# Column-band attention: filler products ahead of PE's waits, the first pair turned in the projection, negated scores, the edge table built between steps

## What is computed

```python
def odd_mixer(x, w_qkv, rel_bias, w_o):
    q, k, v = jnp.split(x @ w_qkv, 3, axis=-1)        # 16 heads of 64
    o = neighbourhood_attention(q.reshape(shp), k.reshape(shp), v.reshape(shp), rel_bias)
    return o @ w_o
...
        k_win = k_band[:, :, :, col_idx]              # 16 columns around each query
        s = jnp.einsum('bhcd,bhicjd->bhcij', q_row, k_win) * scale + bias[None]
        p = jax.nn.softmax(s.reshape(B, H, GRID_W, kh * kw), axis=-1)
        return jnp.einsum('bhcij,bhicje->bhce', p, v_win)
```

## Time and profile before

| | us |
|---|---|
| median of 3 runs | 3365.94 |
| lowest and highest run | 3365.29, 3375.21 |
| the profiled execution | 3375.81 |
| its span | 3374.0 |
| stage of the 32 steps, from the last projection product (1198.8) to the turns of the output (1327.7) | 128.9 |

### The profile page before, as it was taken

How to read it: one execution, slowest core, us unless ns; L and a number is a source line. 1 busy time by engine, 2 the same in 40 slices (tenths; PEclk the granted TensorE clock), 3 DMA queues, 4 the chain that set the end, 5 groups by cost and what they waited for, 6 DMA issues and landing times.

```text
span 3374.0 us, 38858 instructions
## 1 busy us (share of the span) xinstructions
PE 3074.9 (91%) x14511; PEld 2394.2 (71%) x14511; DVE 2173.6 (64%) x2409; ACT 1602.0 (47%) x1889; POOL 405.5 (12%) x274
## 2 busy tenths in 40 slices
PE   8677799999996989699999996998899998999998
PEld 6456666777775867576666765877778887778886
DVE  2375677888884245588888876565367655757753
ACT  2354267777774344277777763443232212732221
POOL 0000121222212000222222212010000000000000
PEclk9898899999998977899999998998999999999999
DMA  7200479999983211489999984330123322223321
GB/s 253 108 1 10 149 303 352 347 363 357 351 333 127 75 44 38 189 322 349 343 357 347 366 303 106 88 75 1 51 75 100 100 100 75 98 84 100 100 93 70
DMA packets 174064, 599.21 MB, mean 178 GB/s; under 512 B 25539, under 2 KB 74867, under 8 KB 124531
## 3 DMA queue, kind: packets, MB, share of 16 engines
q1 hardware_dynamic: 140112, 541.74, 44.0%
q0 software_dynamic: 23472, 51.42, 4.3%
q10 hardware_dynamic: 10355, 4.33, 0.5%
HBM read 581.17 MB, written 48.23 MB: 187 GB/s over the span
## 4 chain that ended last, share of the span: by engine, by line
PE 77%; DVE 7%; DMA 7%; ACT 4%; issue 3%; POOL 1%; DVEq 0%; SPq 0%; ACTq 0%; POOLq 0%
PE bank L1781 22%; PE bank L1783 21%; PE bank L1782 21%; DMA ring<-w_gate 4%; PE bank L2270 2%; PE bank L2037 1%; PE bank L1966 1%; ACT ring_rounded L1235 1%; PE bank L1756 1%; PE bank L1878 1%; PE bank L1854 1%; DVE st L2675 1%; PE bank L2057 1%; DMA big<-expert_rows,idx 1%; PE bank L1936 1%
## 5 line engine op out<-in xcount | busy, mean ns | idle before, releaser
L1782 PE MATMUL bank<-ring_rounded,big_rounded 128*96 128x512 f32 (+1 forms) x1712 | 675.3, 394 | 0.0
L2909 DVE TENSOR_TENSOR ring_rounded<-ring,big_rounded 128x2048 fp32r<-128x2048 f32 x252 | 568.1, 2288 | 39.6 <-ACT big_rounded L1235 38.1
L2565 DVE TENSOR_TENSOR ring_rounded<-ring,ring_rounded 128x2048 fp32r<-128x2048 f32 (+2 forms) x128 | 282.4, 2249 | 409.1 <-ACT ring_rounded L1065 408.9
L1235 ACT ACTIVATE big_rounded<-ring 128x2048 fp32r<-128x2048 f32 x252 | 478.2, 1918 | 66.7 <-DMA ring<-w_up 52.3
L1065 ACT ACTIVATE ring_rounded<-ring 128x2048 fp32r<-128x2048 f32 (+2 forms) x128 | 234.1, 1878 | 453.5 <-DMA ring<-ffn_w_down 164.5
L2909 DVE TENSOR_TENSOR ring_rounded<-ring,ring_rounded 128x2048 fp32r<-128x2048 f32 x128 | 292.8, 2289 | 171.0 <-ACT ring_rounded L1235 162.9
L1781 PE MATMUL bank<-big_rounded 128*96 128x512 f32 x1008 | 401.2, 398 | 0.0
L1783 PE MATMUL bank<-big_rounded,XH_rounded 128*96 128x512 f32 x1008 | 398.3, 395 | 0.0
L1781 PE MATMUL bank<-XT_rounded,ring_rounded 128*128 128x512 f32 x928 | 364.7, 393 | 2.4 <-DVE big L2998 2.4
L1783 PE MATMUL bank<-XT_rounded,ring_rounded 128*128 128x512 f32 x928 | 361.9, 390 | 0.0
L1782 PE MATMUL bank<-XH_rounded,ring_rounded 128*128 128x512 f32 x928 | 361.7, 390 | 0.0
(11 more groups left out here) (419 smaller groups left out, 4549.2 us busy)
## 6 DMA issues: line engine op xcount, KB each, us to landing
ring<-w_up SPq DMA_DIRECT2D x128, 1024.0 KB, 7.9
ring<-w_down SPq DMA_DIRECT2D x128, 1024.0 KB, 8.0
ring<-w_gate SPq DMA_DIRECT2D x128, 1024.0 KB, 7.2
ring<-ffn_w_up SPq DMA_DIRECT2D x44, 1024.0 KB, 6.9
ring<-ffn_w_down SPq DMA_DIRECT2D x10, 2048.0 KB, 8.0
ring<-ret_gdn_w_in SPq DMA_DIRECT2D x8, 2048.0 KB, 12.4
expert_rows<-lnp POOLq DMA_DIRECT2D x1, 12288.0 KB, 39.1
ring<-odd_w_qkv SPq DMA_DIRECT2D x6, 2048.0 KB, 8.0
```

Of the source, the lines that this page charges most:

```text
L1235: act.activation(one_pass(expert_hi(j)), expert_raw(j), ACT.Copy).then_inc(signal("half_rounded").sem, 1)
L1782: pe.matmul(dst, x_hi, y_lo, start=False, stop=False)
L2565: dve.tensor_tensor(one_pass(w), w, parts(hi(c)[:, ks, :]), ALU.subtract).then_inc(split[c.pair], 1)
L2909: dve.tensor_tensor(one_pass(expert_raw(j)), expert_raw(j), parts(expert_hi(j)), ALU.subtract).then_inc(signal("half_split").sem, 1)
```

## The change

- **Fillers.** In each step PE runs one product of the identity with constants ahead of the wait for exp (256 columns) and one ahead of the wait for the copied weights (128 columns). They write to the bank that the real products overwrite; the wait for that bank now comes first.
- **First pair.** The transposes of pair 0 stand ahead of the last row tile of the projection; ACT copies them (`qk_bands(0)`) between the copies of the last two tiles. PE no longer waits for all projection tiles to be copied ahead of the stage, but for the value chunks at steps 0 and 16.
- **Negated scores.** DVE writes minus (scaled score plus bias), takes the minimum, and ACT computes exp of minus that plus the minimum. The separate negation goes.
- **Edge table.** The right-hand table is built in one piece behind step 0's minimum and two behind step 1's; the first pair's bands go 0, 1, 2, 3, those of the others 3, 0, 1, 2.
- **Places.** `p`, the shifted values and a pair's q and k change buffers; the clearing of `p` goes. The shifted values come in two halves, 512 columns each, with a signal of their own.
- **Waits** of ACT and DVE for their own last instruction go where nothing needs them.
- **After the stage** ACT and DVE take the first chunk of output weights in two pieces, ahead of turned tiles 0 and 4.

```diff
-        C["QKT"] = [XT[:, 6:8, :], C["QKT"]]
         spare_rows = lnp[:, :, :].rearrange("p a b -> p (a b)")
-        C["p"] = spare_rows[:, 0:1536].rearrange("p (i m s) -> p i m s", i=3, m=2)
+        C["QKT"] = [[spare_rows[:, 1536:2048], big[:, 16384:16896]], [C["QKT"][:, 0, :], C["QKT"][:, 1, :]]]
+        C["p"] = XT[:, 0:3, :].rearrange("p a s -> p (a s)").rearrange("p (i m s) -> p i m s", i=3, m=2)
         C["shift"] = spare_rows[:, 0:1536].rearrange("p (j i r c) -> p j i r c", j=2, i=4, r=12)
-        C["V2"] = XT[:, 0:6, :].rearrange("p a s -> p (a s)").rearrange("p (t d) -> p t d", t=3)
+        C["V2"] = [spare_rows[:, 0:1536].rearrange("p (t d) -> p t d", t=3), XT[:, 3:6, :]]
...
+        def band(i):
+
+            g = i // T
+            return g, ((0, 1, 2, 3) if g == 0 else (3, 0, 1, 2))[i % T]
...
-                for us in U["qkv"][4:6]:
-                    for u in us:
+                for i, told in ((0, "v2_low"), (1, "v2_high")):
+                    for u in U["qkv"][4 + i]:
                         sp.wait_ge(drained[u.bank], u.n + 1)
-                for half in range(2):
-                    rows = slice(64 - 64 * half, P - 64 * half)
-                    sp.dma_start(C["V2"][64 * half:64 * half + 64, :, :], C["H"][rows, half:half + 3, 2 * D:3 * D]).then_inc(signal("v2_loaded").sem, 16)
+                    cols = slice(2 * D + BANK * i, 2 * D + BANK * (i + 1))
+                    for half in range(2):
+                        rows = slice(64 - 64 * half, P - 64 * half)
+                        sp.dma_start(C["V2"][i][64 * half:64 * half + 64, :, :], C["H"][rows, half:half + 3, cols]).then_inc(signal(told).sem, 16)
...
+                if (i, t) == (5, T - 2):
+                    qk_bands(0)
...
+            def qk_bands(g):
+
+                for j, v in enumerate(U["C"]["qk"][g]):
+                    act.wait_ge(full[v.bank], v.n + 1)
+                    to, by = (from_fours, by_fours) if j == 0 else (bands, grid)
+                    act.activation(to(C["QKT"][g % 2][j]), by(ps(v)[:, :]), ACT.Copy).then_inc(drained[v.bank], 1)
...
-                            ins = act.activation(p, p, ACT.Exp, bias=negmax[:, j:j + 1], accum_out=sums[:, j:j + 1])
+                            p, j = C["p"][:, i % 3, m, band_cols(b)], 2 * i + m
+                            ins = act.activation(p, p, ACT.Exp, bias=negmax[:, j:j + 1], scale=-1.0, accum_out=sums[:, j:j + 1])
                         ins.then_inc(signal("exp_done").sem, 1)
-                        act.wait_ge(signal("exp_done").sem, signal("exp_done").next(act))
-                        if i % T == 2 and i // T + 1 < C_HEADS // 2:
-                            group(i // T + 1)
+                        if i % T == 2 and g + 1 < C_HEADS // 2:
+                            qk_bands(g + 1)
...
+            def back_to_grid(c):
+
+                act.wait_ge(loaded[c.slot], 16 * c.loads)
                 for i, u in enumerate(U["o1_T"]):
+                    if i % 4 == 0:
+                        ks = pieces(c)[i // 4]
+                        act.activation(one_pass(hi(c)[:, ks, :]), raw(c)[:, ks, :], ACT.Copy).then_inc(rounded[c.pair], 1)
                     act.wait_ge(full[u.bank], u.n + 1)
                     act.activation(one_pass(by_fours(XT[:, i, :])), from_fours(ps(u)[:, :]), ACT.Copy).then_inc(signal("xt_rounded").sem, 1)
...
+            def keep_busy(v, n):
+
+                pe.matmul(ps(v)[:, 0:n], ident, const[:, 0:n], start=True, stop=True)
...
                 def turn_weights(i):
                     v = u["t"][i][0]
-                    pe.wait_ge(signal("exp_done").sem, signal("exp_done").next(pe))
                     if v.n:
                         pe.wait_ge(drained[v.bank], v.n)
+                    keep_busy(v, 256)
+                    pe.wait_ge(signal("exp_done").sem, signal("exp_done").next(pe))
                     for m in range(2):
                         for c in range(2):
                             ins = pe.transpose(ps(v)[:, 256 * m + P * c:256 * m + P * (c + 1)], C["p"][:, i % 3, m, P * c:P * (c + 1)], ident)
                     ins.then_inc(full[v.bank], 1)
...
                 def weighted(i):
-                    g, b = i // T, BANDS[i % T]
+                    g, b = band(i)
                     v = u["o"][i][0]
-                    pe.wait_ge(drained[u["t"][i][0].bank], u["t"][i][0].n + 1)
-                    if i == 2:
-                        pe.wait_ge(signal("v2_loaded").sem, signal("v2_loaded").next(pe, 32))
                     if v.n:
                         pe.wait_ge(drained[v.bank], v.n)
+                    keep_busy(v, 128)
+                    pe.wait_ge(drained[u["t"][i][0].bank], u["t"][i][0].n + 1)
+                    if i in (0, n // 2):
+                        told = "v2_low" if i == 0 else "v2_high"
+                        pe.wait_ge(signal(told).sem, signal(told).next(pe, 32))
+                        for w in U["qkv"][4 if i == 0 else 5]:
+                            pe.wait_ge(drained[w.bank], w.n + 1)
...
-                group(0)
                 for i in range(n + 3):
                     if i < n:
                         scores(i)
                         if i % T == 2 and i // T + 1 < C_HEADS // 2:
-                            group(i // T + 1)
+                            turn_qk(i // T + 1)
...
-                linear_chunk(W["qkv"][5], U["qkv"][5], hi_at=feature_rows(x_hi_B), lo_at=feature_rows(XT))
-                for us in U["qkv"]:
+                linear_chunk(W["qkv"][5], U["qkv"][5], tiles=range(T - 1), hi_at=feature_rows(x_hi_B), lo_at=feature_rows(XT))
+                for us in U["qkv"][0:4]:
                     for v in us:
                         pe.wait_ge(drained[v.bank], v.n + 1)
+                turn_qk(0)
+                linear_chunk(W["qkv"][5], U["qkv"][5], tiles=(T - 1,), hi_at=feature_rows(x_hi_B), lo_at=feature_rows(XT))
...
+                        if i == 0:
+                            u5 = U["qkv"][5][T - 1]
+                            dve.wait_ge(full[u5.bank], u5.n + 1)
...
-                            dve.scalar_tensor_tensor(p[:, m, :], ps(v)[:, 0:nk], C_DIM ** -0.5, table[:, m, :], ALU.mult, ALU.add).then_inc(
+                            dve.scalar_tensor_tensor(p[:, m, :], ps(v)[:, 0:nk], -C_DIM ** -0.5, table[:, m, :], ALU.mult, ALU.subtract).then_inc(
                                 drained[v.bank], 1)
                         for v in u["s"][i]:
                             dve.wait_ge(drained[v.bank], v.n + 1)
-                        dve.tensor_reduce(negmax[:, j:j + 2], p, AX_X, ALU.max).then_inc(dve_done.sem, 1)
-                        dve.wait_ge(dve_done.sem, dve_done.next(dve))
-                        dve.tensor_scalar(negmax[:, j:j + 2], negmax[:, j:j + 2], -1.0, None, ALU.mult).then_inc(signal("max_ready").sem, 1)
-                        dve.wait_ge(signal("max_ready").sem, signal("max_ready").next(dve))
-                        if i == 0:
-                            u5 = U["qkv"][5][T - 1]
-                            dve.wait_ge(full[u5.bank], u5.n + 1)
-                            window_table("right", 0)
+                        dve.tensor_reduce(negmax[:, j:j + 2], p, AX_X, ALU.min).then_inc(signal("max_ready").sem, 1)
+                        if i < 2:
+                            window_table("right", 0, ((0,), (1, 2))[i])
...
+            def rest_from_bands(c):
 
                 for i, u in enumerate(U["o1_T"]):
+                    if i % 4 == 0:
+                        w, h = (f(c)[:, pieces(c)[i // 4], :] for f in (raw, hi))
+                        dve.wait_ge(rounded[c.pair], 2 * c.nth - 1 + i // 4)
+                        dve.tensor_tensor(one_pass(w), w, parts(h), ALU.subtract).then_inc(split[c.pair], 1)
...
-                dve.memset(C["p"], 0.0).then_inc(dve_done.sem, 1)
-                dve.wait_ge(dve_done.sem, dve_done.next(dve))
-                window_table("mid", 0)
-                window_table("left", 1)
+                window_table("mid", 0, range(4))
+                window_table("left", 1, range(3))
                 windows()
-                rest_of_chunk(W["odd_o"][0])
-                rest_from_bands()
+                rest_from_bands(W["odd_o"][0])
```

51 lines of the change are left out of this document (19 added, 32 removed).

## The result

The changed kernel takes **3341.77 us** (median of 5 runs, 3338.47 to 3351.62) where the kernel before, run beside it, takes 3365.94 (5 runs, 3365.29 to 3375.21): 24.2 us less by the medians. The ratio over all runs is 0.9922 with the interval 0.9907 to 0.9937, which is 26 us less, 21 to 31. The profiled execution of after took 3351.6, against 3375.8 before: 24.2 us less, where 16.4 were forecast.

The account below looks back on a forecast made before the run. PE bounds the column-band attention, at a granted clock of 0.69. Gains of 2.9 (start), 10.7 (steps) and 3.0 (end), less 0.2 (tail), sum to 16.4 us: 3349.5 from the median 3365.9, range 3342 to 3361.

Parts of the forecast that it names:

- the fillers hold the clock: Column-band attention: fillers at 0.65 us a step at full clock keep PE's clock up once it is up.
- The steps: The 25 steps from scores 6 to scores 31: 79.0 us instead of 89.65, a gain of 10.7.
- the end: From scores 31 to the turns of the output: 9.6 us instead of 12.6, a gain of 3.0.
- Rival 2: Clock keeps falling in the stage and fillers are paid at half speed: 12 us slower, 3378; chance 0.11.
- Rival 1: Clock holds, but fillers cost 1.0 or the chain asks 3.5 a step: gain 8, 3358; chance 0.12.
- Rival 3: Fillers free but useless, clock swings as now, only the start gains: 3 us faster, 3363; chance 0.03.
- self-waits of ACT and DVE removed: off the path, 0: ACT and DVE no longer wait for their own last instructions: claimed off the path, gain 0.
- The pair: First pair turned ahead of the last projection tile: scores 0 start at about 1200.0 instead of 1202.18, gain 2.2.
- the negations: Separate negation on DVE goes: three lie on the path in steps 0 to 2, gain 0.6; later 0.
- Clock at the start: First steps' fillers cost 1.3 more each at half speed, while the clock should rise sooner: 0, bounds -4 to +1.
- Tail: After the last step, output weights rounded in two pieces between ACT's and DVE's copies: -0.2, bounds -1.5 to +1.
- Tables and the memset: Right-hand edge table split between steps: about 0; memset gone and window tables earlier, where DVE idles: 0.

Follow-up runs that it names:

- no_fillers: The changed kernel with both fillers of each step left out: 3360.49 us (10 runs), ratio 0.9969 to the kernel before.
- negation_back: The changed kernel with positive scores, the maximum and the separate negation put back: 3354.58 us (one run).
- pair_in_stage: The changed kernel with the first pair's transposes and copies put back behind the last projection tile: 3350.82 us (one run).
- table_whole: The changed kernel with all three pieces of the right-hand edge table behind step 0: 3350.99 us (one run).
- dose_full: The changed kernel plus three fillers of 256 columns and three of 512 in PE's idles at step 0, each step's fillers kept: 3344.57 us.
- after_again: The changed kernel unaltered, profiled once more: 3344.95 us, ratio 0.9935 to the kernel before.
- the dose: Three more fillers of 256 columns and three of 512 at step 0, added to the changed kernel; with its full step fillers 3344.57 us.

## Why the prediction was right, and where not

- **What bounds the stage, and that the fillers hold the clock: right, and shown** by taking them away (0.69) and by adding them alone (0.90, with 1.00 once up). The steps were priced at 79.0 and took 78.67; the end at 9.6 and took 9.60. That the sum came out so near is in part luck: in four steps of after (1235.11 to 1247.66, 12.55) the fillers took 3.05 where 2.60 was priced, while turns, the pair and the weighted products took 0.57 less than priced. A filler of 256 columns costs 0.43 behind the pair's transposes (1223.51 to 1223.94) and 0.54 behind scores (1226.78 to 1227.32), but then the turns behind it take 0.44 instead of 0.50; the 128-column one 0.22 (0.32 where a 64-row product follows). The drain after the scores is only moved, as the forecast had it. No wait is left in the steps.
- **Rival 2 (the swing goes on): fell.** Low for 7 of 110 us, where it needed 28%; and turns hold the clock as products do. **Rival 1** (3.5 a step): a step took 3.15. **Rival 3** (fillers free but useless): fell with no_fillers, whose stage is 15.5 us longer.
- **The step that failed: the start was mis-sized,** and in it the term "self-waits of ACT and DVE removed: off the path, 0". Forecast were 2.9 at the first weighted product, measured 3.7 (16.34 - 11.70 - 0.93), and 4.6 at scores 6. The pair gave 2.0 for 2.2 and the negations 0.6 for 0.6; 1.1 stands where the forecast had 0.1 for the rest. ACT, from the exp of step 2 to the copy that the first weighted product waits for, before and then after:

```profile
1212.09 0.51 ACT L1159 ACTIVATE lnp<-lnp,st 128x256 f32<-128x256 f32 x1 [1.00 <-DVE st L2743]
...
1213.21 1.23 ACT L1149 ACTIVATE big<-bank 128x512 f32<-128x512 f32 x2
1214.47 0.60 ACT L1169 ACTIVATE big<-bank 128x512 f32<-128x512 f32 x1
```

```profile
1209.97 0.51 ACT L1164 ACTIVATE XT<-XT,st 128x256 f32<-128x256 f32 x1 [2.94 <-DVE st L2762]
...
1210.97 1.06 ACT L1153 ACTIVATE big<-bank 128x512 f32<-128x512 f32 x2
1211.92 0.59 ACT L1173 ACTIVATE big<-bank 128x512 f32<-128x512 f32 x1
```

  From that exp to the first weighted product it was 3.03 before (1212.09 to 1215.12) and is 2.60 after (1209.97 to 1212.57), all of it ACT's own work in a row, on the path. The 0.43 lies at the three places where ACT no longer waits for its own last instruction, 0.13 to 0.15 at each. The exp's new scale is not the cause: negation_back has the old exp and the short 2.60. On DVE, whose tables and scores lie ahead on the same path, the next instruction starts 0.12 sooner at three places where such a wait went (0.08 behind the start of a negation or a reciprocal in negation_back, 0.20 before), and between the two copies of the first pair another 0.14 goes (0.63 before, 0.49 in pair_in_stage). Together that is 0.9 of the 1.1 for a term put at nothing. The waits were not put back alone, and the tiles lie in other buffers too, so this rests on the rows, not on a run of its own.
- **Clock at the start, 0 with bounds -4 to +1: a gain of 0.9,** from the first weighted product to scores 6 (10.3 before, 9.4 after); in table_whole and negation_back it was a loss of 1.6 to 1.8 against before. It is inside its bounds, and it is the part of the stage that varied most. That it can be had whole was shown by dose_full: scores 6 at 18.3 instead of 21.1.
- **Tail: a loss of 0.2 forecast, a gain of 0.3 measured** (10.47 to 10.16), 0.2 of it by the order. "DVE is late next" was right.
- **Tables and the memset: 0, right** at the first weighted product. The two loads of V2 on SP held nothing up: no wait of PE in the steps.
- **The sum and the footing.** The sum per stage missed by 2.5 us (18.9 for 16.4): 0.8 at the first weighted product, 0.9 by the clock up to scores 6, 0.5 in the tail, 0.3 in the steps. With 18.9 the forecast would have been 3347.0, and a range moved along with it would have held the time. The other 5.2 us between the profiles, 6.4 behind the stage less 1.2 ahead of it, lie in unchanged code, which behind the stage takes 2025.7 to 2035.9 in three profiles of before alone. The range had only the terms of the stage in it, nothing for the scatter of the kernel itself (before: 3353 to 3385 over all runs) or of a median of few runs; with a time 0.2 us outside, which side of its end the time fell on is also chance.
- **What stays open:** the ratios mean 22 to 26 us, and the stage explains 19 to 23 of them, by which profile of before one takes (139.4 or 143.2). The last few us aren't settled. Behind the stage, after and after_again (2029.5 and 2026.2) lie within what before itself takes, so that the unchanged stages only wander fits; a small gain in them isn't excluded.

## What to carry to other kernels

Where PE's busy time is high at a low granted clock, price each step at both levels and look for the wait at which the clock falls; an f32 product with the identity in that wait, 0.2 to 0.5 us, turned 3.6 us a step into 3.15 here. First fill the idle after which the clock first falls: it cost nothing here, where PE waited anyway, and then two thirds or a third of the filler held the clock in the profiled executions. Price an engine's waits for its own last instruction (0.12 to 0.15 us each here) wherever that engine's work lies in a row on the path. Put the scatter of unchanged stages between two profiles of the same kernel into the range, beside the bounds of the terms.

## What the runs showed of the hardware that was not expected

- Fillers that are f32 transposes hold the clock as well as products of the same length: 0.97 over the stage in both, 0.69 in the steps with none.
- A filler that holds a high clock doesn't by that raise a low one soon: with 128 columns a step it stayed at 0.52 for some 37 us though PE was busy 37.8 of 38, then at 1.00 for the rest with the same steps; and with the dose ahead the same filler ran at 1.00 from the first step.
- A wait of an engine for its own last instruction costs 0.12 to 0.15 us: ACT's copies in a row start 0.63 apart with it and 0.48 without. This is read off the rows of before and after; no run puts the waits back alone.
- The same steps of the same kernel meet the fall at different moments in different executions: before's last low stretch was 24 us in two profiles and 44 in a third, and its 25 steps took 89.7, 89.6 and 92.4.
- An f32 product of 64 columns costs 0.17 where one of 128 costs 0.22, and slows what follows by 0.05. No run here shows what sets this floor.
